# Expert rows returned inside the filter-spectra stage, with its tables loaded during the last expert pass

## The reference, cut to what matters

```python
def moe_swiglu(h, router, wg, wu, wd):          # the end of the first block
    top_v, top_i = lax.top_k(logits, TOP_K)     # 2 of 8 experts for each token
    gates = jax.nn.softmax(top_v, axis=-1)
    ...
    for e in range(N_EXPERTS):
        y = y + combine[..., e:e + 1] * swiglu(h, wg[e], wu[e], wd[e]).astype(jnp.float32)
...
    x = x + y.astype(x.dtype)
    return rmsnorm(x, final_norm)               # what the second block starts from
```

## Time and profile before

| | us |
| --- | --- |
| median of three runs | 2919.02 |
| lowest, highest | 2915.22, 2928.09 |
| the profiled execution | 2917.68 |
| its span | 2915.9 |

### The profile page before, as it was taken

The page is one execution under the profiler, slowest core; times in us unless marked ns, Lnnn a source line. Parts: engine busy times, 40 slices in busy tenths (PEclk is TensorE's granted clock), DMA queues, the critical chain, the costliest instruction groups (busy, mean ns, idle before and its releaser), DMA issues. The chain is left out here.

```text
span 2915.9 us, 43813 instructions
## 1 busy us (share of the span) xinstructions
PE 2779.7 (95%) x17995; PEld 2459.6 (84%) x17995; DVE 1980.1 (68%) x1922; ACT 1506.8 (52%) x1439; POOL 75.1 (3%) x66
## 2 busy tenths in 40 slices
PE   7999999899999999999996899999999899999999
PEld 6799998688888888888883788999999788999898
DVE  6655575588888888888874765666555666665554
ACT  3443454477777677776762326443433235444442
POOL 1000000000000000000001200000000100000000
PEclk8999999899999999999997999999999999999999
DMA  6255550899999999999994343444355343443453
GB/s 193 73 183 193 175 159 17 320 396 370 363 382 357 385 365 362 382 356 385 366 365 152 109 129 103 145 145 145 121 185 187 122 127 106 147 143 131 143 188 104
DMA packets 370551, 639.90 MB, mean 219 GB/s; under 512 B 15096, under 2 KB 201558, under 8 KB 369124
## 3 DMA queue, kind: packets, MB, share of 16 engines
q1 hardware_dynamic: 367704, 628.02, 62.0%
q10 hardware_dynamic: 1550, 5.57, 0.5%
q0 software_dynamic: 1152, 4.19, 0.4%
HBM read 618.22 MB, written 19.53 MB: 219 GB/s over the span
## 5 line engine op out<-in xcount | busy, mean ns | idle before, releaser
L369 DVE TENSOR_TENSOR slots_low<-slots,w_hi 128x2048 fp32r<-128x2048 f32 x240 | 550.7, 2298 | 380.1 <-ACT w_hi L358 379.7
L358 ACT ACTIVATE w_hi<-slots 128x2048 fp32r<-128x2048 f32 x240 | 452.6, 1890 | 336.4 <-PE ps L952 174.4
L1311 DVE TENSOR_TENSOR slots_low<-slots,w_hi 128x2048 fp32r<-128x2048 f32 x224 | 503.4, 2286 | 72.3 <-ACT w_hi L1263 72.3
L471 PE MATMUL ps<-x_hi_low,w_hi 128*128 128x256 f32 x1520 | 435.9, 287 | 32.9 <-DVE x_lo_low L556 15.3
L471 PE MATMUL ps<-x_lo_low,w_hi 128*128 128x256 f32 x1520 | 428.9, 282 | 0.0
L471 PE MATMUL ps<-x_hi_low,slots_low 128*128 128x256 f32 x1520 | 428.8, 282 | 0.0
L1263 ACT ACTIVATE w_hi<-slots 128x2048 fp32r<-128x2048 f32 x224 | 417.0, 1910 | 13.6 <-DMA slots<-in_moe_w_up_dram 8.2
L1200 PE MATMUL ps<-slots_low,x_hi_low 128*128 128x512 f32 x896 | 351.6, 392 | 0.0
L471 PEld LDWEIGHTS ps<-x_hi_low,w_hi 128*128 128x128 f32 x1520 | 292.6, 192 | 39.9 <-issue 30.6
L471 PEld LDWEIGHTS ps<-x_lo_low,w_hi 128*128 128x128 f32 x1520 | 292.7, 193 | 0.3
L471 PEld LDWEIGHTS ps<-x_hi_low,slots_low 128*128 128x128 f32 x1520 | 292.8, 193 | 0.0
(11 more groups left out here) (525 smaller groups left out, 5226.7 us busy)
## 6 DMA issues: line engine op xcount, KB each, us to landing
slots<-in_moe_w_gate_dram SPq DMA_DIRECT2D x112, 1024.0 KB, 5.4
slots<-in_moe_w_up_dram SPq DMA_DIRECT2D x112, 1024.0 KB, 6.0
slots<-in_moe_w_down_dram SPq DMA_DIRECT2D x112, 1024.0 KB, 5.6
slots<-in_mlp_w_dram SPq DMA_DIRECT2D x64, 1024.0 KB, 5.3
slots<-in_w_in_dram SPq DMA_DIRECT2D x54, 1024.0 KB, 5.3
slots<-in_ffn_w_gate_dram SPq DMA_DIRECT2D x14, 1024.0 KB, 5.0
slots<-in_ffn_w_up_dram SPq DMA_DIRECT2D x14, 1024.0 KB, 5.0
slots<-in_ffn_w_down_dram SPq DMA_DIRECT2D x14, 1024.0 KB, 4.9
```

Source lines behind the costliest of these rows:

```text
L358: act.activation(w_hi[:, s.buffer, 0:s.kt * s.cols], slots[:, s.slot, 0:s.kt * s.cols], ACT.Copy).then_inc(w_hi_done, 1)
L369: dve.tensor_tensor(slots_low[:, s.slot, 0:n], slots[:, s.slot, 0:n], w_hi[:, s.buffer, 0:n].bitcast(F32), ALU.subtract).then_inc(w_lo_don ...
L471: mm = pe.matmul(b[:, t * T:(t + 1) * T], w, xx[:, k, :], **flags)
L1311: dve.tensor_tensor(low[i % NS], raw[i % NS], his[i % R].bitcast(F32), ALU.subtract).then_inc(lo_done, 1)
```

## The change

The return of the rows leaves the experts' stage and goes into the stage of the spectra. There the gathers write into a part of `w_hi` that is free (`back`), and `ab` (`sizes` before) lies in another part of it. GpSimd issues the first token half's two gathers as soon as the last store is in, ahead of unit 0's zeroed value, and the second half's two behind it. Weighting and adding stand at the end of unit 0, the transposes (`turn_rows`) and the additions to `res` at the end of unit 2. ScalarE's squares stand in unit 3, and the sums over the width, the root, the reciprocal and the eight scalings come after unit 3. The split of the first slab moves from unit 3 to unit 1.

The hidden values, `hy_w`, its bias rows, `hy_window` and a copy of `dft` get fixed places at the top of SBUF. SP issues their seven DMAs (`load_tables`) between the last slab of the last pass and the first slab of the next section. `dft` is loaded once more to its old place for later stages. The matmuls on zeros at the end are 40 instead of 28. The wait of the next stage for the stored spectra moves from ScalarE to VectorE and GpSimd.

```diff
@@ experts @@
                     n = passes(sp, body)
+                    load_tables(sp)
                     for s in range(AHEAD):
                         sp.wait_ge(used, SLABS * n + s + 1)
                         fetch(sp, after + s)
...
-                    sp.dma_start(block_of_rows(y_rows, n), y[:, :]).then_inc(stored, 16)
+                    sp.dma_start(block_of_rows(y_rows, n), y[:, :]).then_inc(last_stored, 16)
...
-                    pool.wait_ge(stored, 16 * n + 16)
...
-                    for t in range(TT):
-                        for k in range(2):
-                            pool.indirect_dma_start(back[:, t, k, :], None, y_flat, bass.IndirectOffsetOnAxis(ap=places[:, 1, k, t:t + 1], axis=0)).then_inc(back_in[t], 16)
+                    pool.memset(h2[64:65, :, :], 1.0)
@@ spectra, vector @@
+                            if i == 0:
+                                for t in range(TT):
+                                    dve.wait_ge(weighed, t + 1)
+                                    dve.scalar_tensor_tensor(out=back[:, t, 0, :], in0=back[:, t, 1, :], scalar=gg[:, t, 3:4], in1=back[:, t, 0, :],
+                                                             op0=ALU.mult, op1=ALU.add).then_inc(rows_joined, 1)
+                            if i == 1:
+                                split_lo(dve, BEFORE_MOE, len(stream.slabs))
                             dve.wait_ge(summed, i + 1)
                             dve.tensor_scalar(filter_size[:, 1, 4 * i:4 * i + 4], bank(4)[:, 0:4], EPS, None, ALU.add).then_inc(sized, 1)
+                            if i == N - 2:
+                                dve.wait_ge(rows_turned, 1)
+                                for b in range(4):
+                                    dve.tensor_tensor(flat(res[:, 2 * b:2 * b + 2, :]), flat(res[:, 2 * b:2 * b + 2, :]), bank(b), ALU.add).then_inc(returned, 1)
+                        dve.wait_ge(means_made, 1)
+                        dve.tensor_scalar(ms[:, :], bank(0)[:, 0:T], 1.0 / D, EPS, ALU.mult, ALU.add).then_inc(shifted, 1)
...
+                        dve.wait_ge(rooted, 1)
+                        dve.reciprocal(ms[:, :], ms[:, :]).then_inc(root_inverted, 1)
+                        dve.wait_ge(root_inverted, 1)
+                        scale_tiles(range(KD))
@@ spectra, gpsimd @@
+                        pool.wait_ge(last_stored, 16)
+                        fetch_rows(0)
                         for i in range(N):
                             pool.wait_ge(windowed, 4 * i + 4)
                             pool.memset(fb[0:1, 1, 0, :], 0.0).then_inc(lag0, 1)
+                            if i == 0:
+                                fetch_rows(1)
@@ spectra, scalar @@
                             for s in range(2):
+                                if i == N - 1:
+                                    act.wait_ge(returned, 2 * s + 2)
+                                    act.activation(sq[:, 4 * s:4 * s + 4, :], res[:, 4 * s:4 * s + 4, :], ACT.Square).then_inc(squared, 1)
                                 act.wait_ge(transformed, 4 * i + 2 * s + 1)
...
@@ load_tables @@
+                def load_tables(sp):
+                    sp.wait_ge(hidden_out, 16)
+                    sp.dma_start(flat(h2[0:64, :, :]), hidden_dram).then_inc(spectra_in, 16)
+                    for l in range(2):
+                        sp.dma_start(w3s[l][0:64, :], A["hy_w3_2"][l]).then_inc(spectra_in, 16)
+                        sp.dma_start(w3s[l][64:65, :], A["hy_b3_2"][l].rearrange("(a n) -> a n", a=1)).then_inc(spectra_in, 16)
+                    sp.dma_start(window[:, :], A["c_hy_window"]).then_inc(spectra_in, 16)
+                    sp.dma_start(first_dft[:, :], A["c_dft"]).then_inc(spectra_in, 16)
```

136 lines of the change are left out of this document (60 added, 76 removed).

## The result

The changed kernel takes 2898.23 us, the median of six runs (2896.56 to 2905.24), where the kernel before takes 2919.66 (2913.91 to 2928.09). The ratio is 0.9926, with a 95% interval of 0.9912 to 0.9940: 21.4 us less. The forecast was 2901, a gain of 17.5.

The account below looks back on a forecast made before the run. TensorE, 95% busy, was taken to idle behind the rows' chain, barrier and table loads. Gains and losses 33.1 - 4.8 - 1.0 - 1.8 - 2.1 - 5.9 = 17.5 us gave 2901 us, range 2890 to 2909.

Parts of the forecast that it names:

- start less gates, 33.1 - 4.8: Start of the stage: unit 0's `make` 33.1 us earlier, less 4.8 for waiting on store and memory input.
- half clock in that `make`: Unit 1's `make`: TensorE, idle since about 1537, runs part of it at 1.2 GHz, costing about 1.0 us.
- unit 0, `make` 1 to `sized`, without it: Unit 1's `make` to unit 0's `sized`: three scalings go, two weightings come; 15.5 us against 13.7, loss 1.8.
- units 1 and 2: Unit 0's `sized` to unit 2's: scalings go, split enters unit 1; 22 us against 19.9, loss 2.1.
- The gates: Before unit 1's `make`: store pushed back 6.7 us to 1542.4; zeroed value and memory input then come together near 1545.
- the barrier: Start of the stage: SP has only the last store to issue, so it falls near 1533.4 instead of behind 1552.5.
- The collision of weighting and addition: Unit 0: VectorE's weightings and GpSimd's addition hold each other up; 15.5 us with it, 13.1 without.
- The tail: Unit 2's `sized` to the next stage: transposes, sums, reciprocal, scalings; 15.7 to 17.8 us, taken 16.7 against 10.8, loss 5.9.
- Rival 1: Last store not pushed back, gates at 1539 to 1540; gain up to 24.2 us, time 2895; chance 0.20.
- Rival 2: TensorE at half clock over much of the stage, costing 8 to 9 us; time 2909; chance 0.16.
- Rivals 3 and 4: 3: time not freed, 2915 to 2919, chance 0.04; 4: slower, last store landing after 1560, chance 0.03.

Follow-up runs that it names:

- rows_undone: Changed kernel with tables still early, but rows fetched, weighted, added, turned and summed ahead of unit 0's `make`; stretch 92.0 us, median 2923.55, ratio 1.0032.
- tables_late: Changed kernel with `load_tables` issued after the barrier, right behind the memory input; stretch 86.1 us, median 2914.50, ratio 0.9977.
- sized_first: Changed kernel with `sized` ahead of the weightings and the split in each unit; stretch 73.2 us, 2893.83 us in one run.
- tables_free: Changed kernel with tables loaded in the idle DMA time before the experts, partly from ScalarE's queue; stretch 62.8 us, median 2890.41, ratio 0.9895.
- clock_held: Changed kernel with matmuls on zeros after unit 0's `make` and ahead of units 1 and 2's transforms; stretch 70.4 us, 2889.57 us in one run.
- tables_first: Changed kernel with `load_tables` issued before the first slab of the first expert pass; stretch 66.7 us, median 2901.99, ratio 0.9938.

## Why the prediction was right, step by step

| step | forecast | measured |
| --- | --- | --- |
| `make` of unit 1 after the copy of `y` (start less gates, 33.1 - 4.8) | 16.8, gain 28.3 | 16.8, gain 28.2 |
| half clock in that `make` | loss 1.0 | loss 0.9 |
| unit 0, `make` 1 to `sized`, without it | 15.5, loss 1.8 | 14.6, loss 0.9 |
| units 1 and 2 | 22, loss 2.1 | 22.3, loss 2.4 |
| `sized` of unit 2 to the next stage | 16.7, loss 5.9 | 15.7, loss 4.8 |
| sum | 17.5 | 19.2 |

**The gates** are the heart of it, and held to 0.1 us. The store was pushed back by the tables and landed in 9.8 us (forecast 9 to 10), and the memory input behind it and the zeroed value came together. That the store's place in the queue is the cause is shown by three kernels: landing in 3.0 and 3.1 us with the tables elsewhere, 6.4 on another queue. `rows_undone` and `tables_late` show that neither half would have done.

**One step was wrong on the way**: the barrier was put at 1.5 us after the copy of `y`, "now SP has only the last store to issue". It fell at 4.0. SP issues late when its queue is full: the store took 2.65 us to issue instead of 0.36. The 2.5 us had no price that shows: `make` still ended before the memory input came, and that landed 2.5 us behind the store, about what its 1 MB takes at the 392 GB/s of that stretch, so it came through a queue that was full anyway. In `sized_first`, where the slabs kept SP for nearly 5 us beyond the copy of `y`, the same effect moved the whole stage.

**The half clock** was there, from 1542.5 to about 1556, and cost 0.9 us. In `tables_free` unit 1's `make`, in the row at 1552.18 above, took 3.60 us at full clock instead of 4.51, and `sized` came 14.6 us behind its start:

```profile
1566.80 0.15 DVE L1528 TENSOR_SCALAR filter_size<-ps 128x4 f32<-128x4 f32 x1
```

In `clock_held`, with the same 3.60, it is 14.6 as well, and in `tables_first`, with 4.01, 15.0. The pair of weightings takes 4.55 or 4.56 us in all of them. So the term of 1.0 was right, and the 15.5 of unit 0, which the forecast gave without the half clock, was 0.9 too long. That unit 0 measured just 15.5 is the sum of both, and luck. The collision of weighting and addition is part of it: the forecast counted 2.4 us for it (15.5 less 13.1), and the pair shows 2.1 (4.55 where it takes 2.47 without). `sized` waited for it, as forecast.

**Units 1 and 2.** The forecast had 12.4 us for unit 1 at full clock and 14.2 at half. It took 13.8 with part of `transform` at half clock, and 12.4 in `clock_held` at full.

**The tail** was 1.0 too long in the forecast. Of the 15.7 to 17.8 given, both with the sums of squares at full clock, it took the middle; the two ends are the transposes of the rows at full and at half clock. They ran at full (1.95 us, until 0.4 behind `sized`), and so did unit 3's `transform` and the sums (3.70 us), so the lower end came. Unit 0 and the tail make the error of 1.7 us (0.9 and 1.0, with 0.1 for the half clock, less 0.3 in units 1 and 2). The median's gain of 21.4 has 2.2 us beyond the stretch, which no step of the forecast covers and which two executions of one kernel differ by as well.

**The rivals.** Rival 1, the store not pushed back, did not happen. It priced what is left on the table at 6.7 us, and two runs lie on either side: the stretch is 3.6 us shorter in `tables_first`, where the clock fell, and 7.5 in `tables_free`, where it held. Rival 2, half clock in much of the stage, was half true. Part of each transform had it (5.22 and 5.16 us), the sums of squares not. It priced 1.8 us for each, and `clock_held` shows 1.3 for the one of unit 1; the forecast's 22 us for units 1 and 2 already held a part of that. For unit 2 no run shows the price, since the fillers ahead of it cost more than they won. Rivals 3 and 4 fell: the next stage started at once, and the store landed 11 us after the copy of `y`, far from the 28 at which the sign turns.

## What to carry to other kernels

When two chains end in the same place, price the move of one by where the other then ends: here one alone brought 3.4 us and the other -2.5, and both 19.2. A load that is moved forward to hide it is put in front of everything that is issued behind it on the same queue; look for a stretch with a DMA share near zero rather than for one in which the engines are idle (here 500 to 518 us, 7.8 us better in the median). A small step that lets another engine go should stand ahead of long work on its engine, not behind it: `sized` ahead of the weightings and the split was worth 3.4 us.
